# A two-block network on one core: the modulation product weighed and added up on GpSimd, summed over partitions on TensorE

## What is computed

```python
# second block; N_MOD = 6, D = 1024: w_mod is 1024 x 6144
mod_l = silu(c) @ w_mod + b_mod          # all six parts are used: sh1, sc1, g1, sh2, sc2, g2
mod_c = silu(c_ctx) @ w_mod + b_mod      # only sh1c and sc1c are used (the first 2048 columns)
pl = modulate(rmsnorm(xl), sh1, sc1) @ w_in
pc = modulate(rmsnorm(xc), sh1c, sc1c) @ w_in
xl = xl + g1 * (concat(ml_l, hg_l) @ w_out)
xl = xl + g2 * conv_ffn(modulate(rmsnorm(xl), sh2, sc2))
```

## Time and profile before

| | before |
|---|---|
| median of 3 runs | 2077.9 us (2074.66 to 2089.6) |
| the profiled execution: its time, its span | 2077.58 us, 2075.7 us |
| PE busy | 1926.9 us (93%) |
| DVE, ACT, POOL busy | 1010.5, 700.4, 401.1 us |
| chain that ended last | PE 80%, DVE 10%, ACT 4%, issue 3%, DMA 2% |

### The profile page before, as it was taken

How to read it: one execution, slowest core, us unless ns; L and a number is a source line. 1 busy time by engine, 2 the same in 40 slices (tenths; PEclk the granted TensorE clock), 3 DMA queues, 4 the chain that set the end, 5 groups by cost and what they waited for, 6 DMA issues and landing times.

```text
span 2075.7 us, 20749 instructions
## 1 busy us (share of the span) xinstructions
PE 1926.9 (93%) x7602; PEld 1280.8 (62%) x7602; DVE 1010.5 (49%) x1877; ACT 700.4 (34%) x1142; POOL 401.1 (19%) x376
## 2 busy tenths in 40 slices
PE   7997779899999899999998998999998989999996
PEld 3556433333787687888773445666564558888874
DVE  5955332221444443244221315656575268777774
ACT  3261223422323343124124214361634153323323
POOL 2621100000200000000000011322222037555551
PEclk9995878999999999999999999999999989999999
DMA  5263342132433132332310221121201134242411
GB/s 134 82 98 95 110 146 81 62 101 76 128 91 111 61 101 81 101 100 84 100 61 1 76 57 41 46 56 31 61 21 41 42 103 122 79 122 68 116 41 41
DMA packets 203020, 164.55 MB, mean 79 GB/s; under 512 B 17527, under 2 KB 193379, under 8 KB 202667
## 3 DMA queue, kind: packets, MB, share of 16 engines
q1 hardware_dynamic: 197803, 149.21, 24.3%
q0 software_dynamic: 4576, 14.17, 3.3%
q10 hardware_dynamic: 560, 0.12, 0.0%
HBM read 153.78 MB, written 4.26 MB: 76 GB/s over the span
## 4 chain that ended last, share of the span: by engine, by line
PE 80%; DVE 10%; ACT 4%; issue 3%; DMA 2%; ACTq 0%; POOLq 0%; POOL 0%; DVEq 0%; SPq 0%
PE bank L1387 25%; PE bank L1722 17%; PE bank L1484 9%; PE bank L1496 4%; PE bank L1277 4%; PE bank L1317 2%; PE bank L1331 2%; DVE arena L2382 2%; PE bank L1169 2%; PE bank L1609 2%; PE bank L1601 2%; PE bank L1083 1%; DMA ring<-in_w_mod 1%; PE bank L1253 1%; PE bank L1077 1%
## 5 line engine op out<-in xcount | busy, mean ns | idle before, releaser
L3189 DVE SCALAR_TENSOR_TENSOR arena<-bank,ffn_taps,arena 128x441 f32<-128x441 f32 (+2 forms) x352 | 220.0, 684 | 81.0 <-ACT arena L2344 81.0
L2752 DVE TENSOR_TENSOR w_lo<-ring,w_hi 128x2048 fp32r<-128x2048 f32 x52 | 119.2, 2292 | 166.0 <-ACT w_hi L1949 161.9
L1484 PE MATMUL bank<-hT,ring 128*128 128x512 f32 x448 | 197.5, 594 | 0.0
L1387 PE MATMUL bank<-h_lo,w_hi 128*128 128x512 f32 x448 | 176.5, 394 | 8.1 <-ACT arena L1986 4.9
L1949 ACT CAST w_hi<-ring 128x2048 fp32r<-128x2048 f32 x52 | 99.1, 1906 | 192.0 <-PE bank L1387 192.0
L1387 PE MATMUL bank<-hT_hi,w_hi 128*128 128x512 f32 x384 | 151.6, 395 | 5.6 <-DVE h_lo L2826 5.6
L1722 PE MATMUL bank<-hT_hi,w_hi 128*128 128x512 f32 x352 | 138.5, 393 | 9.9 <-DVE h_lo L3167 9.9
L1484 PEld LDWEIGHTS bank<-hT,ring 128*128 128x128 f32 x448 | 84.0, 191 | 97.5 <-issue 97.3
L1387 PE MATMUL bank<-act_hi,w_hi 128*128 128x512 f32 x352 | 137.8, 391 | 5.4 <-DVE act_lo L2838 5.4
L1033 POOL TENSOR_TENSOR w_lo<-ring,w_hi 128x2048 fp32r<-128x2048 f32 x22 | 101.7, 4624 | 187.9 <-ACT w_hi L2318 124.7
L1722 PE MATMUL bank<-h_lo,w_hi 128*128 128x512 f32 x352 | 138.0, 392 | 0.0
(11 more groups left out here) (455 smaller groups left out, 3674.3 us busy)
## 6 DMA issues: line engine op xcount, KB each, us to landing
ring<-in_w_up SPq DMA_DIRECT2D x76, 512.0 KB, 4.6
ring<-in_w_mod SPq DMA_DIRECT2D x48, 512.0 KB, 4.6
ring<-in_w_in SPq DMA_DIRECT2D x72, 256.0 KB, 3.3
ring<-in_w_down SPq DMA_DIRECT2D x32, 512.0 KB, 4.0
ring<-in_w_in SPq DMA_DIRECT2D x30, 512.0 KB, 4.1
arena<-in_w_down SPq DMA_DIRECT2D x22, 512.0 KB, 4.5
ring<-in_w_out SPq DMA_DIRECT2D x8, 512.0 KB, 4.1
ring<-in_w_out SPq DMA_DIRECT2D x16, 256.0 KB, 3.0
```

The costliest lines, as they stand in the source:

```text
L1387: ins = pe.matmul(out, u[:, n % SLOTS, cols], v[:, k, :], start=start and k == w[0][0] and m == 0, stop=stop and k == w[-1][0] and m == 2)
L1484: ins = pe.matmul(o, w[:, k, :], src[:, k, 0:n], start=k == 0, stop=k == DT - 1)
L2752: ve.tensor_tensor(w_lo[:, n % SLOTS, :], ring[:, n % SLOTS, :], value(w_hi[:, n % SLOTS, :]), ALU.subtract)\
L3189: return ve.scalar_tensor_tensor(o[:, ys, xs], x[:, yt, xt], ffn_taps[:, at:at + 1], o[:, ys, xs], ALU.mult, ALU.add)
```

## The change

The product of a chunk moves from PE to POOL. For each chunk POOL multiplies the eight slabs in the ring slot by their column of `silu_c` in place (eight `tensor_scalar` of 128 x 256), adds them up in a tree (1024, 512 and 256 columns) and leaves 128 x 256 in `mod_sums`. For the first eight chunks (BOTH_MODS), whose columns are used for c_ctx too, it first makes a running sum for v = 1, with a wait behind each of its 15 instructions. PE then takes the sum over the partitions: `mod_sums` as the stationary operand (128 x 128) and a column of ones as the moving one, 4 products per chunk for the first eight and 2 for the others, each giving one column of `mod_bank`, which now holds all 64 columns to the end. Copies, stores, the reload and the flip are gone; the bias is added at s = 70 of the item loop, and the last `glu` waits for it. A chunk's load now waits for `mod_summed` instead of `chunk_used`. The tables of places are new.

```diff
-MOD_AFTER = {1: 0, 3: 1, 5: 2, 9: 3, 11: 4, 13: 5, 15: 6, 17: 7}
+MOD_AFTER = {5: 0, 11: 1, 17: 2}
-CMP_MODS = 8
-MOD_AT = {3 + 4 * k: 9 + k for k in range(8)} | {37 + 4 * k: 17 + k for k in range(7)}
+BOTH_MODS = 2 * DT // 2
+MOD_AT = {2: 3, 4: 4, 7: 5, 13: 6, 19: 7} | {23 + 3 * k: BOTH_MODS + k for k in range(MODS - BOTH_MODS)}
+MOD_DONE = max(MOD_AT) + 2
...
             for c in range(MODS):
-                columns(C0["mod"] + c, a["w_mod_2"][0], c * width, width)
-                if c:
-                    store_mod(c - 1)
+                if c == 1:
+                    sp.wait_ge(hid_full, 2)
+                elif c:
+                    sp.wait_ge(mod_summed, c - 1)
+                columns(C0["mod"] + c, a["w_mod_2"][0], c * width, width, free=c > 0)
...
+            sp.wait_ge(mod_summed, MODS - 1)
+            load(g, (dst[:, 0:2], w_glu[:, 0:2]), (dst[:, 2:4], w_glu[:, 2:4]), free=True)
+            sp.wait_ge(mod_summed, MODS)
...
+            def sum_mod(c):
+                n = C0["mod"] + c
+                pool.wait_ge(loaded[n % SLOTS], 32 * (n // SLOTS + 1))
+                if c >= 2:
+                    pool.wait_ge(mod_taken, c - 1)
+                w = ring[:, n % SLOTS, :].rearrange("p (k n) -> p k n", k=DT)
+                sums = mod_sums[:, c % 2]
+                if c < BOTH_MODS:
+                    step(pool.tensor_scalar(sums[:, 1], w[:, 0, :], silu_c[:, 0, 1:2], None, ALU.mult))
+                    for k in range(1, DT):
+                        step(pool.tensor_scalar(sums[:, 0], w[:, k, :], silu_c[:, k, 1:2], None, ALU.mult))
+                        step(pool.tensor_tensor(sums[:, 1], sums[:, 1], sums[:, 0], ALU.add))
+                for k in range(DT):
+                    last = step.mark(pool.tensor_scalar(w[:, k, :], w[:, k, :], silu_c[:, k, 0:1], None, ALU.mult))
+                step.wait(last)
+                step(pool.tensor_tensor(w[:, 0:4, :], w[:, 0:4, :], w[:, 4:8, :], ALU.add))
+                step(pool.tensor_tensor(w[:, 0:2, :], w[:, 0:2, :], w[:, 2:4, :], ALU.add))
+                ins = pool.tensor_tensor(sums[:, 0], w[:, 0, :], w[:, 1, :], ALU.add)
+                ins.then_inc(mod_summed, 1)
...
+            sum_mod(0)          # behind the swap of z, ahead of the masks
...
+            for c in range(1, 3):
+                sum_mod(c)      # behind the masks, ahead of the wait for y_copied
...
+            sum_mod(3)          # behind y_scr, ahead of y_us and yT
...
+            for c in range(4, MODS):
+                sum_mod(c)      # behind yT, ahead of the context
...
-            for k in range(2):
-                pool.wait_ge(mod_stored[k], 16 * MODS // 2)
-            pool.dma_start(mod_back[0:2 * NMOD * DT], mod_scr.rearrange("c (m p) -> (c m) p", p=P)).then_inc(mod_in, 16)
...
             def modulation(c):
+                pe.wait_ge(mod_summed, c + 1)
+                for v in range(2 if c < BOTH_MODS else 1):
+                    for k in range(2):
+                        at = v * NMOD * DT + 2 * c + k
+                        ins = pe.matmul(mod_bank[:, at:at + 1], mod_sums[:, c % 2, v, k * P:(k + 1) * P], one[:],
+                                        start=True, stop=True)
+                ins.then_inc(mod_taken, 1)
```

More of the change, by code:

```diff
@@ L653, in _, with load @@
             skipped = [0]
-            def load(n, *pairs, i=0, per=0, split=None):
-                if split is not None:
+            def load(n, *pairs, i=0, per=0, split=None, free=False):
+                if free:
+                    pass
+                elif split is not None:
                     sp.wait_ge(split_ready, split + 1 + i * per)
@@ L1360, in _ @@
                 rows_of(h)
-            modulation(CMP_MODS)
             for s in range(AHEAD):
```

72 lines of the change are left out of this document (24 added, 48 removed).

## The result

The changed kernel takes 2208.67 us (median of four runs, 2206.19 to 2211.5) where the kernel before, run beside it, takes 2080.95: ratio 1.061, 95% interval 1.057 to 1.065. It is slower by 128 us. The forecast was 2042 us, range 2014 to 2086. In the two profiled executions the spans are 2209.8 and 2075.7 us, and the 134.1 us between them fall into two parts at the first merge product: 638.88 - 525.72 = 113.2 us ahead of it, 1570.9 - 1550.0 = 20.9 us behind it.

The account below looks back on a forecast made before the run. PE's own list was taken to bound the item loop, and POOL the stage after the change. First merge product at 459.6 + 27.7 + 3 = 490.3 us, 35.4 earlier: 2077.6 - 35.4 = 2042 us, range 2014 to 2086.

Parts of the forecast that it names:

- The price of `tensor_scalar` (0.40, start to start 0.36): POOL's weighing of 128 x 256, priced from the select rows; chunks of 16.1 us early and 7.4 us late, 247 us together.
- Rival A: POOL's `tensor_scalar` costs as much as a two-input instruction: 301 us of chunks, 2096 us, not faster; 9 in 100.
- Rival D: Early chunks delayed by waits; slower from 20 us per early chunk on, 2154 us at 30 us each; 5 in 100.
- 142 us instead of 197: PE's own need in the item loop up to the first glu: 128 us plus 14 us of new products.
- 2 us for a colder clock: Stage end, from first glu to first merge product: 2 us added for a lower PE clock after its wait.
- The lead of 39 us: Start of the item loop: first part near 262 us instead of 300.9.
- The merge stage and all behind it only move: Stages from the merge on: they start earlier but keep their length, a change of nothing.
- 27.7 + 3 us: First glu to first merge product: 27.7 us as before, plus 1 for new products and 2 for a colder clock.
- Rivals B: Cheap end: `tensor_scalar` at 0.32 us on POOL and little contention, 2015 us, within 2008 to 2026; 15 in 100.
- E: No gain, since PE in the loop was held by other engines; 2 in 100.
- Contention (5 us: POOL's sums slowed by a busy DVE beside them: 5 us chosen, with 0 and 37 us as bounds.
- rival C: POOL and DVE stop one another for whole instructions: POOL 31 us later, 2068 us, or 2074 at 15%; 12 in 100.

Follow-up runs that it names:

- experiment 5: Eight old-form long products, result unused, put back ahead of PE's wait from the fourth chunk on: changed kernel 2213.15 us (ratio 1.062), kernel of experiment 4 2114.53 us.
- experiment 4: Changed kernel with all of GpSimd's sums left out but the last add of each chunk: 2090.46 us, ratio 1.000; with the one-column tensor behind the arena 2065.58 us.
- experiment 7: Kernel of experiment 4 with the one-column tensor behind the arena and eight unused long products ahead of chunks 3 to 7 only: 2068.08 us, ratio 0.992.
- experiment 6: Kernel before with two instead of eight products in each of chunks 9 to 23, nothing put in their place: 2061.56 us, ratio 0.990.
- experiments 3: Changed kernel without the second weighted sum of the first eight chunks on GpSimd: 2156.65 us, ratio 1.034.

## Why the prediction was wrong

**The price of `tensor_scalar` (0.40, start to start 0.36).** This step failed first. It is 0.90, so 256 x 0.54 = 138 us on POOL's list. The first chunk took 30.2 us and the other early ones 25.6 to 26.2 instead of 16.1 (ends of the first three at 232.2, 259.7, 285.6; forecast 216.5, 234.7, 250.8), late ones mostly 11.8 instead of 7.4. Chunk 22 was summed at 602.9 instead of 455, and this is why the first merge product came at 638.9 instead of 490.3. My upper bound of 0.61 came from another kind of instruction and bounded nothing: one input is dearer than two. Rival A had the right mechanism, but stopped its price at that bound. Rival D had the right threshold (over 20 us per early chunk, slower than before) and 5 in 100, but thought of waits as the cause; these were 0.08 to 0.10 us, as in the sum.

**"142 us instead of 197", PE's own need in the loop, and "2 us for a colder clock".** This step failed too. It cost the changed kernel nothing that experiment 5 could find, since POOL set the end there, but it bounds what the idea can give with any price. I took the duration of PE's items from a loop at 0.90. Without the long products the items ran at 0.50 to 0.57 (experiment 4), and a list of 142 us filled the old time and more: 210.9 us in the profile of experiment 7, with 19 us of added products, against 197.1 before. The lead of 39 us at the loop's start shrank as well, to 11 us there (first part at 289.9, not 262), at a clock of 0.50 to 0.53 from 200 us on. The gain with a free GpSimd is 23 us (ratio 0.989: 0.011 x 2080), not the 55 of the shorter list and the 39 of the earlier start. I had read the clock of 0.84 in the earlier trace rows as a matter of waits. Experiment 4 has no waits at a clock of 0.50, experiment 6 has all waits of before at 0.79.

**"The merge stage and all behind it only move."** Failed by 20.9 us, of which 17.9 went away with the place of one tensor of one column (1570.9 to 1553.0); the other 3.0 are within what old-placement kernels show (1549.1 to 1553.5).

**What held.** POOL is the bound and PE follows it: 95.2 us of waits on its last add. Loads and `mod_taken` were hidden (1.0 us of waits). The end of the stage, 27.7 + 3 us from the first glu to the first merge product, took 638.88 - 608.21 = 30.67. New products of PE took 28.9 us instead of 19, off the path. Rivals B and E fell.

**Contention (5 us, rival C).** Rival C's mechanism is in the trace, but small. Most adds and `tensor_scalar` of the stage kept one price to the end (2.35, 1.26, 0.90), and the largest exceptions stand beside long products of VectorE like the two shown. Added up over the chunks, what they took beyond the shortest of their kind (25.55 and 11.75 us), less the 1.0 of waiting, is some 10 us, an estimate that puts all of it on VectorE: twice the 5 that I chose, and far from C's 31.

**The account.** Of 134.1 us between the profiles, 20.9 lie behind the merge's start, 17.9 of them placement. Ahead of it are 113.2, which are the 148.6 of delay against the forecast less the 35.4 of gain in it. POOL's list has this delay: chunk 23 was summed at 614.7 instead of 462.6, 152 us late, of which `tensor_scalar` is 138, the 80 adds of 256 columns (0.72 instead of 0.61) are 9, and contention is 5 more than allowed. Taken away in turn, the first merge product comes 61.3 us earlier without the weighing's price and 54.2 without the second sums. With all sums but the last add gone the median falls by 118 us (2208.67 to 2090.46), of which its profile, taken in a long execution, shows 96 (638.9 to 542.5). That even then the kernel is no faster than before (ratio 1.000) is the placement (0.989 without it) and the clock.

## What to carry to other kernels

A price must be measured on the engine and for the operation in question; a neighbour that looks dearer is no upper bound, and a single added instruction in an idle stretch settles it for nothing. Before taking long products off TensorE, ask at what clock the rest will run: here 39 us of products removed gave 21, and 40 us replaced by another engine's sums gave none that could be measured. And compare the mean of an untouched product in both profiles: one column allocated ahead of the big operands moved them and cost the changed kernel 17 us (ratio 1.061 against 1.053 with the column behind them). In the kernel before, the same move cost the stretch 17 us and the whole nothing that could be measured, so this is to be tried, not assumed.

## What the runs showed of the hardware

- On GpSimd `tensor_scalar` costs 0.28 us and 2.5 ns a column, a copy 0.37 us for 256 columns, a two-input product of 128 x 2048 with a broadcast operand 3.61 us (1.8 ns a column), less than the add of two full inputs of the same size (4.62).
- TensorE can be busy in 100.00 of 100 us by its records and be granted 1.2 GHz all through. The Trainium skill (TensorE: Matmul & The Clock Gate, HAM oscillation — how this bites in real kernels) ties the loss of the clock to idle gaps; experiments 3 and 4 show it without any, and in experiment 5 the clock came back with long products alone. Which property of the 128 x 64 and 67-row products of the item loop fails to raise it was not tried.
- Moving the float32r operands by 32, 64 or 96 bytes in their partitions made 128 x 512 products up to 8 ns of 395 slower, 17 us over a stretch of 1550; moved by 128 bytes it was 8 us. The time of the whole kernel before changed by 0.1 to 0.7%, and not measurably with 32 or 128 bytes.
- GpSimd instructions of 256 columns that take 0.92 and 0.72 us took 2.81 and 2.16 beside products of VectorE of 2016 columns with both inputs in SBUF.
